# A top-2 mixture of experts on one core: tiles of 128 slots with one expert each become tiles of two 64-slot halves, each with its own expert

## The chip, the cores and the metric

The kernel runs on one core of a Trainium2 chip. The metric is the device time in microseconds (us) of one execution. Everything is computed in 32-bit floats; most matrix products, those of the experts among them, are plain fp32 products, each of which the trace shows as two weight loads and two matmul records.

The engines are named as the profile names them: PE (TensorE, matmul), PEld (its weight loads), DVE (VectorE), ACT (ScalarE), POOL (GpSimd), SP (SyncE, which here issues most DMAs). SBUF is the on-chip memory, PSUM the accumulator that PE writes. PEclk is the share of full TensorE clock that was granted.

## The reference

One layer of a decoder trunk: a gated linear recurrence and a differential attention over 1104 tokens (16 meta tokens, 64 sample tokens, 1024 prompt tokens), merged and projected, and then the part that the change is about, a mixture of 16 small MLPs. Each token goes to one group of four experts and, inside it, to the best two experts:

```python
g_idx = jnp.argmax(g_logits, axis=-1)
top_p, top_i = lax.top_k(e_prob, TOP_K)                 # TOP_K = 2, inside the chosen group of 4
gate = p_g * top_p / jnp.sum(top_p, axis=-1, keepdims=True)
eid = g_idx[..., None] * EXPERTS_PER_GROUP + top_i
h = jax.nn.silu(jnp.einsum('btd,edf->btef', x, w_gate)) * jnp.einsum('btd,edf->btef', x, w_up)
return jnp.einsum('btef,efd->btd', h * combine[..., None].astype(h.dtype), w_down)
```

`D_MODEL` is 1024 and the width of an expert 256, so an expert has 1024x256 numbers in each of `w_gate` and `w_up` and 256x1024 in `w_down`, 3 MB in all. 1104 tokens times two experts are 2208 assignments. Worked out from the reference's inputs, experts 0 to 15 get 144, 126, 82, 114, 209, 155, 153, 209, 114, 130, 162, 134, 114, 103, 117 and 142 of them.

## The kernel before

The program is a row of phases, each a block in which every engine has its own instruction stream: the first norm, the recurrence, prompt attention, sample attention, the merge, the output projection (`phase_output`), the routing (`phase_route`), the experts (`phase_experts`) and the copy of the results (`phase_results`). The change lies in the last but two and the last but one.

**Routing.** `phase_route` finds each token's two experts on DVE, counts the tokens of each expert, and gives every assignment a slot. A tile is 128 slots of one expert; an expert with n tokens gets n/128 tiles, rounded up. The arrays `token` (row to fetch), `dest` (row to add to), `slot_weight` (the gate, 0 in an empty slot), `expert` and `buffer` (expert of a tile, modulo 4) and `ends` (the number of tiles up to and with expert e) hold the plan. SP loads the weights of the first four experts meanwhile, and POOL gathers the rows of the first two tiles.

**A tile.** In `phase_experts` PE runs `step` for tile j (`par` = j modulo 2 picks the buffers):

1. the product for gate and up of tile j (L2208), 8 pieces of 128 rows by 512 columns, into PSUM bank 2 + par. It waits for `xt_done` (the turned rows are in SBUF) and for `weights_ready`;
2. the turn of tile j + 1 (L2185), 8 transposes;
3. the down product of tile j - 1 (L2195), 4 pieces of 512 columns, which ends with an increment of `y_made`;
4. the turn of the hidden values of tile j (L2179), which waits for `h_done`.

ACT follows with `silu` (L2235), `result` (L2241, half of the down product of the tile before, out of PSUM) and `hidden` (L2245); DVE with `hidden` (L2280, up times silu times gate), `place` (L2276, the turned rows to SBUF) and `result` (L2287). POOL gathers rows (L2086) and adds a tile's output rows to the running sum in DRAM (L2141). A token's two experts are in different tiles, and the additions of a tile wait for those of the tile before.

**Weights.** There are four buffers of expert weights. SP's program, L2121 to L2135, sets when a buffer is filled and when its content is announced. `say_ready(e)` waits until the three DMAs of expert e have landed and then raises `weights_ready` by one:

```python
for e in range(BUFFERS - 2):
    say_ready(e)
for e in range(BUFFERS, E):
    say_ready(e - 2)
    ends = sp.value_load(K["ends"][0:1, e - BUFFERS:e - BUFFERS + 1], min_val=0, max_val=SLOTS)
    sp.wait_ge(y_made, ends + 1)
    load_expert(sp, A, K, e, e % BUFFERS)
for e in range(E - 2, E):
    say_ready(e)
```

`y_made` starts at 1, so the wait is for the down product of the last tile of expert e - 4.

Tiles are run in pairs; with the counts above there are 25 tiles, so 26 run, the last one empty.

Of the kernel before, what the change touches and what calls it, by code (L numbers as in the profile page):

```python
# [49 lines left out]
SLOTS = (2 * TOK - E) // P + E + 1  # L50
# [5 lines left out]
FEWEST = -(-2 * TOK // P)  # L56
# [25 lines left out]
def constants():  # L82
# [40 lines left out]
    c["experts"] = np.broadcast_to(np.concatenate([np.arange(4, 0, -1), 128.0 * np.arange(9), np.arange(P)]).astype(np.float32), (P, 13 + P)).copy()  # L123
# [8 lines left out]
def build(nc, A, out):  # L132
    with ExitStack() as stack:
# [70 lines left out]
        K["expert"], K["buffer"], K["token"], K["dest"], K["ends"], K["before_last"] = (sb(n).bitcast(I32) for n in (SLOTS, SLOTS, SLOTS, SLOTS, E, 1))  # L204
        K["slot_weight"] = sb(SLOTS)
        top[0] = 0
# [1672 lines left out]
def phase_route(nc, A, K, sb, psum):  # L1879
# [3 lines left out]
    with ExitStack() as st:  # L1883
# [4 lines left out]
        bias, consts, strict, ones, tok, valid, emask = sb(20), sb(13 + P), sb(P), sb(P), sb(NT), sb(NT), sb(E, NT)  # L1888
# [7 lines left out]
        inc, cmp9, ntile, incl, excl, sm = sb(E, NT), sb(E, NT), sb(E), sb(E), sb(E), sb(NT, E)  # L1896
        lt, eid, eidb, step, last = sb(SLOTS, E), sb(SLOTS), sb(SLOTS), sb(SLOTS), sb(1)
# [4 lines left out]
        pri, steps128, jj, lanes = consts[:, 0:4], consts[:, 4:13], consts[:, 13:13 + SLOTS], consts[:, 13:13 + P]  # L1902
# [37 lines left out]
        def _(dve):  # L1940
# [42 lines left out]
            for j in range(2):  # L1983
                dve.tensor_tensor(OH[j].rearrange("p n (g e) -> p n g e", g=G), ohg.unsqueeze(3).to_broadcast([P, NT, G, PE_]),
                                  oh[j].unsqueeze(2).to_broadcast([P, NT, G, PE_]), ALU.mult)
# [20 lines left out]
            dve.tensor_tensor(cmp9, inc[:, :, NT - 1:NT].to_broadcast([P, E, NT]), steps128.unsqueeze(1).to_broadcast([P, E, NT]), ALU.is_gt)  # L2006
            D_()
            dve.tensor_reduce(ntile, cmp9, AX_X, ALU.add)
# [7 lines left out]
            dve.tensor_scalar(excl, excl, float(P), None, ALU.mult)  # L2016
# [41 lines left out]
            dve.tensor_tensor(lt, incl.unsqueeze(1).to_broadcast([P, SLOTS, E]), jj.unsqueeze(2).to_broadcast([P, SLOTS, E]), ALU.is_le)  # L2058
# [6 lines left out]
            dve.tensor_copy(K["ends"], incl)  # L2065

            dve.tensor_tensor(step[:, 0:SLOTS // 2 - 1], consts[:, 15:13 + SLOTS:2], incl[:, E - 1:E].to_broadcast([P, SLOTS // 2 - 1]), ALU.is_lt)
# [22 lines left out]
def load_expert(sp, A, K, e, b):  # L2090
# [6 lines left out]
def phase_experts(nc, A, K, sb, psum):  # L2097


    with ExitStack() as st:  # L2100
# [9 lines left out]
        hg, hT, Y = [sb(FF) for _ in range(2)], [sb(2, P) for _ in range(2)], [sb(D) for _ in range(2)]  # L2110
        block = st.enter_context(nc.Block())
        PAIRS = SLOTS // 2

# [58 lines left out]
        def _(pe):  # L2172
            def buffer_of(j):
                return pe.value_load(K["buffer"][0:1, bass.ds(j, 1)], min_val=0, max_val=BUFFERS - 1)
# [13 lines left out]
            def down(j, par, first, b):  # L2188
                pe.wait_ge(ht_done, j + 1)
                if not first:  # L2190
                    pe.wait_ge(y_act, j)
                    pe.wait_ge(y_dve, j)
                for n in range(2):
                    for k in range(2):
                        mm = pe.matmul(psum[:, 5 + n, :], hT[par][:, k, :], K["Wd"][:, bass.ds(2 * b + k, 1), 512 * n:512 * n + 512], start=(k == 0), stop=(k == 1))  # L2195
                mm.then_inc(y_made, 1)

            def step(i, par, first=False, end=False):
# [3 lines left out]
                e = pe.value_load(K["expert"][0:1, bass.ds(j, 1)], min_val=0, max_val=E - 1)  # L2202
# [29 lines left out]
        def _(act):  # L2232
# [13 lines left out]


            silu(0, 0)
# [113 lines left out]
```

## Time and profile before

| | us |
|---|---|
| three runs | 1891.2, 1893.44, 1904.81 |
| median | 1893.44 |
| the profiled execution, its own time | 1894.98 |
| its span in the trace | 1893.3 |

| engine | busy us | share of the span |
|---|---|---|
| PE | 1619.3 | 86% |
| DVE | 638.8 | 34% |
| ACT | 470.0 | 25% |
| POOL | 256.4 | 14% |

The experts' phase runs from about 1554 us to about 1864 us; after it come the last additions to the running sum and the copy of the results. In the rows, a line such as L2208 is line 2208 of the kernel before; x16 counts records, so a plain fp32 product counts twice; in brackets stands the idle time of that engine just before, and what ended it.

### The profile page before, as it was taken

To read this page: it belongs to the slowest core of one execution; us is meant where nothing else is said; L and a number is where in the kernel's file an instruction comes from. 1 tells how busy PE (TensorE), PEld (TensorE's weight loads), DVE (VectorE), ACT (ScalarE), POOL (GpSimd) and SP (SyncE) were. 2 spreads that over 40 slices of the span, in tenths; PEclk is the share of its full clock that TensorE was granted. 3 is DMA by queue.
4 is the path that set the end of the run, shared out by engine and by line. 5 is a ranking of instruction groups with operands and counts; after the bars stand their busy time and mean duration, and the time that the engine had idled before them with its cause. 6 is when DMAs were issued, how large, how long until landed. Compare 5 with 4: busy or idle time off the path is not lost. (4 is left out here: it accounts for less than half of the span.)

```text
span 1893.3 us, 25322 instructions
## 1 busy us (share of the span) xinstructions
PE 1619.3 (86%) x9005; PEld 1068.2 (56%) x9006; DVE 638.8 (34%) x1496; ACT 470.0 (25%) x1158; POOL 256.4 (14%) x455
## 2 busy tenths in 40 slices
PE   5998889966898989896576899999899829999993
PEld 4554445544465656554354788888678724444441
DVE  4345454454244544444231311111132241112210
ACT  2233333333233434343122211011132200111110
POOL 1000101011222222221322000000000001222211
PEclk8999899986898999998797999999999959999997
DMA  6001200000302020000983221111143294989755
GB/s 210 1 1 57 69 1 25 1 25 3 96 1 58 1 58 1 24 1 24 318 302 97 77 67 34 34 34 34 49 140 101 100 304 132 305 233 272 223 144 128
DMA packets 135893, 179.08 MB, mean 95 GB/s; under 512 B 9427, under 2 KB 106966, under 8 KB 135702
## 3 DMA queue, kind: packets, MB, share of 16 engines
q1 hardware_dynamic: 123126, 131.47, 21.8%
q0 software_dynamic: 12608, 44.05, 8.7%
q10 hardware_dynamic: 48, 2.10, 0.3%
q8 instruction: 68, 1.11, 0.3%
q14 instruction: 43, 0.35, 0.1%
HBM read 146.72 MB, written 35.32 MB: 96 GB/s over the span
## 5 line engine op out<-in xcount | busy, mean ns | idle before, releaser
L979 PE MATMUL psum<-branch_part,kept 128*128 128x384 f32 (+1 forms) x576 | 198.2, 499 | 1.5 <-DVE branch_part L1210 1.5
L2208 PE MATMUL psum<-moe_part,kept 128*128 x416 | 185.9, 600 | 5.9 <-DVE kept L2276 3.4
L979 PEld LDWEIGHTS psum<-branch_part,kept 128*128 128x128 f32 (+1 forms) x576 | 106.8, 190 | 75.4 <-issue 14.2
L487 PE MATMUL psum<-kept,branch_part 128*128 128x368 f32 x384 | 127.5, 489 | 8.1 <-PEq L224 5.1
L1644 PE MATMUL psum<-split 128*128 128x368 f32 x384 | 133.3, 347 | 0.0
L1638 PE MATMUL psum<-kept,merge_part 128*128 128x368 f32 x384 | 124.2, 476 | 9.6 <-DMA merge_part<-w_da_out 9.6
L2208 PEld LDWEIGHTS psum<-moe_part,kept 128*128 128x128 f32 x416 | 77.7, 192 | 95.7 <-issue 94.9
L492 PE MATMUL psum<-branch_part,kept 128*128 128x512 f32 (+1 forms) x288 | 129.3, 604 | 1.5 <-DVE kept L701 1.5
L1645 PE MATMUL psum<-split 128*128 128x368 f32 x384 | 126.9, 331 | 0.0
L1646 PE MATMUL psum<-split 128*128 128x368 f32 x384 | 126.6, 330 | 0.0
L1693 DVE TENSOR_TENSOR merge_part<-merge_part,psum 128x368 f32<-128x368 f32 x48 | 23.6, 534 | 252.8 <-ACT merge_part L1669 252.8
L487 PEld LDWEIGHTS psum<-kept,branch_part 128*128 128x128 f32 x384 | 74.2, 197 | 53.4 <-issue 10.5
L1638 PEld LDWEIGHTS psum<-kept,merge_part 128*128 128x128 f32 x384 | 72.9, 191 | 50.9 <-DMA merge_part<-w_da_out 10.0
L2195 PE MATMUL psum<-moe_part,kept 128*128 x208 | 93.7, 593 | 0.9 <-ACT kept L2245 0.9
L492 PEld LDWEIGHTS psum<-branch_part,kept 128*128 128x128 f32 (+1 forms) x288 | 54.2, 192 | 67.2 <-issue 64.9
L1669 ACT ACTIVATE merge_part<-psum 128x368 f32<-128x368 f32 x48 | 20.3, 474 | 276.1 <-PE psum L1646 276.1
L1002 PE MATMUL psum<-branch_part 128*128 128x512 f32 (+3 forms) x192 | 76.3, 514 | 0.0
L2280 DVE SCALAR_TENSOR_TENSOR kept<-kept,moe_part,psum 128x256 f32<-128x256 f32 x26 | 12.5, 481 | 186.7 <-ACT kept L2235 186.7
L1358 PE MATMUL psum<-kept,branch_part 128*128 128x128 f32 x256 | 45.5, 332 | 34.3 <-DMA branch_part<-cache_k 21.8
L1644 PEld LDWEIGHTS psum<-split 128*128 128x128 f32 x384 | 72.2, 188 | 2.9
L1645 PEld LDWEIGHTS psum<-split 128*128 128x128 f32 x384 | 72.1, 188 | 2.9
L1038 PE MATMUL psum<-branch_part 128*128 128x128 f32 (+2 forms) x360 | 60.2, 310 | 15.7 <-DVE branch_part L1210 14.1
(326 smaller groups left out, 2575.1 us busy)
## 6 DMA issues: line engine op xcount, KB each, us to landing
branch_part<-cache_k SPq DMA_DIRECT2D x64, 256.0 KB, 5.8
branch_part<-cache_v POOLq DMA_DIRECT2D x64, 256.0 KB, 5.2
moe_part<-w_gate SPq DMA_DIRECT2D x16, 1024.0 KB, 6.5
moe_part<-w_up SPq DMA_DIRECT2D x16, 1024.0 KB, 12.7
moe_part<-w_down SPq DMA_DIRECT2D x16, 1024.0 KB, 13.8
branch_part<-w_in SPq DMA_DIRECT2D x8, 1024.0 KB, 8.3
merge_part<-w_in SPq DMA_DIRECT2D x16, 512.0 KB
branch_part<-w_in SPq DMA_DIRECT2D x12, 512.0 KB
```

Source lines behind the costliest of these rows:

```text
L487: mm = pe.matmul(bank[:, 0:CH], Wb[0][:, k, c0:c0 + P], K["xT"][:, k, CH * i:CH * i + CH], start=(k == 0), stop=(k == KC - 1))
L492: mm = pe.matmul(bank[:ROWS[i], :], K["xT"][:, k, cols(i)], Wb[1][:, k, :], start=(k == 0), stop=(k == KC - 1))
L979: mm = pe.matmul(bank_of(("z", h, i))[:ROWS[i], 0:384], K["xT"][:, k, cols(i)], Wb[h % 2][:, k, :], start=(k == 0), stop=(k == KC - 1))
L1002: mm = pe.matmul(lg[m][:r, c:c + w], q, kT[h % 2][:, FIRST + c:FIRST + c + w], start=True, stop=True)
L1038: mm = pe.matmul(bank_of(("o", s, 0))[:r, 0:P], aT[:w, n, :r], v[h % 2][:w, 0 if n == i else n + 1, :], start=(n == 0), stop=(n == i))
L1358: mm = pe.transpose(psum[:, 3 + n % 2, P * h:P * h + P], Kp[b2][:, n % NPG, P * h:P * h + P], K["ident"])
L1638: pe.matmul(banks[2 + j], Wy[c % 2][:, k, P * j:P * j + P], src[:, k, chunk(n)], start=(k == 0), stop=(k == HEADS - 1))
L1644: pe.matmul(banks[j], wh[c % 2][:, k, ch], xh[:, k, chunk(n)], start=(k == 0), stop=False)
L1645: pe.matmul(banks[j], wh[c % 2][:, k, ch], xl[:, k, chunk(n)], start=False, stop=False)
L1646: mm = pe.matmul(banks[j], wl[c % 2][:, k, ch], xh[:, k, chunk(n)], start=False, stop=(k == KC - 1))
L2195: mm = pe.matmul(psum[:, 5 + n, :], hT[par][:, k, :], K["Wd"][:, bass.ds(2 * b + k, 1), 512 * n:512 * n + 512], start=(k == 0), stop=(k == 1))
L2208: mm = pe.matmul(psum[:, 2 + par, :], XT[par][:, k, :], K["GU"][:, bass.ds(KC * b + k, 1), :], start=(k == 0), stop=(k == KC - 1))
```

## The change

**The tile.** A tile still has 128 slots, but they are two halves (`groups`) of 64, and each half has an expert of its own. An expert with n tokens gets n/64 halves, rounded up, and the halves follow one another without a gap, so that an expert can end in the first half of a tile and the next begin in the second.

**The order of the experts.** They are taken in the order 0, 4, 8, 12, 1, 5, 9, 13, 2, 6, 10, 14, 3, 7, 11, 15. Neighbours are of different groups, and a token's two experts are of one group, so the two halves of a tile never hold the same token and a tile's rows can be added in one indirect DMA. By the counts above the halves per expert in this order are 3, 4, 2, 2, 2, 3, 3, 2, 2, 3, 3, 2, 2, 4, 3, 3, together 43.

**The products.** Each matmul of a tile becomes two: one with the weights (stationary side: the 64 turned rows) of slots 0 to 63 into PSUM partitions 0 to 63, one with slots 64 to 127 into partitions 64 to 127. The first reads the expert's weights in their buffer; the second reads a copy in `GU2` and `Wd2`, made per tile by ACT (`copy_gate`, 6 of the 8 rows of 512, two instructions) and DVE (`copy_up`, 2 of the 8 rows; `copy_down`, 2048 columns). The copies of a tile are made even where both halves have one expert.

**The plan.** `expert` and `buffer` have an entry per half, `ends` is the number of tiles up to and with the tile in which an expert ends.

```diff
+GROUPS = 2
+GROUP = P // GROUPS
+ENTRIES = (2 * TOK - 2) // GROUP + E
+SLOTS = -(-ENTRIES // (2 * GROUPS)) * 2
+NSTEP = -(-TOK // GROUP)
+CUT = 6
...
+            dve.tensor_scalar(ends, incl, 1.0 / GROUPS, 0.5 - 0.5 / GROUPS, ALU.mult, ALU.add)
...
-def load_expert(sp, A, K, e, b):
+def load_expert(sp, A, K, turn, b):
+
+    e = 4 * (turn % 4) + turn // 4
...
+        def second_of(e, j):
+
+            x = e.value_load(K["expert"][0:1, bass.ds(2 * j + 1, 1)], min_val=0, max_val=E - 1)
+            b = e.value_load(K["buffer"][0:1, bass.ds(2 * j + 1, 1)], min_val=0, max_val=BUFFERS - 1)
+            e.wait_ge(weights_ready, x + 1)
+            return b
...
             def down(j, par, first, b):
                 pe.wait_ge(ht_done, j + 1)
+                pe.wait_ge(down_copied, j + 1)
...
-                        mm = pe.matmul(psum[:, 5 + n, :], hT[par][:, k, :], K["Wd"][:, bass.ds(2 * b + k, 1), 512 * n:512 * n + 512], start=(k == 0), stop=(k == 1))
+                        pe.matmul(psum[0:64, 5 + n, :], hT[par][:, k, 0:64], K["Wd"][:, bass.ds(2 * b + k, 1), 512 * n:512 * n + 512],
+                                  start=(k == 0), stop=(k == 1))
+                        mm = pe.matmul(psum[64:128, 5 + n, :], hT[par][:, k, 64:128], Wd2[par][:, k, 512 * n:512 * n + 512],
+                                       start=(k == 0), stop=(k == 1))
...
+                pe.wait_ge(gate_copied, j + 1)
+                pe.wait_ge(up_copied, j + 1)
                 for k in range(KC):
-                    mm = pe.matmul(psum[:, 2 + par, :], XT[par][:, k, :], K["GU"][:, bass.ds(KC * b + k, 1), :], start=(k == 0), stop=(k == KC - 1))
+                    pe.matmul(psum[0:64, 2 + par, :], XT[par][:, k, 0:64], K["GU"][:, bass.ds(KC * b + k, 1), :],
+                              start=(k == 0), stop=(k == KC - 1))
+                    mm = pe.matmul(psum[64:128, 2 + par, :], XT[par][:, k, 64:128], GU2[par][:, k, :],
+                                   start=(k == 0), stop=(k == KC - 1))
...
+            def copy_gate(j, par, first=False):
+                b = second_of(act, j)
+                if not first:
+                    act.wait_ge(gu_done, j - 1)
+                for k in range(0, CUT, 3):
+                    ins = act.activation(GU2[par][:, k:k + 3, :], K["GU"][:, bass.ds(KC * b + k, 3), :], ACT.Copy)
+                ins.then_inc(gate_copied, 1)
...
             with act.Fori(1, PAIRS - 1) as i:
                 with act.If(i < last):
+                    copy_gate(2 * i + 2, 0)
                     silu(2 * i + 1, 1)
                     result(2 * i, 0, i)
                     hidden(2 * i + 1, 1)
+                    copy_gate(2 * i + 3, 1)
                     silu(2 * i + 2, 0)
...
+            def copy_up(j, par, first=False):
+                b = second_of(dve, j)
+                if not first:
+                    dve.wait_ge(gu_done, j - 1)
+                dve.tensor_copy(GU2[par][:, CUT:KC, :], K["GU"][:, bass.ds(KC * b + CUT, KC - CUT), :]).then_inc(up_copied, 1)
+
+            def copy_down(j, par, first=False):
+                b = second_of(dve, j)
+                if not first:
+                    dve.wait_ge(y_made, j)
+                dve.tensor_copy(Wd2[par], K["Wd"][:, bass.ds(2 * b, 2), :]).then_inc(down_copied, 1)
...
             with dve.Fori(1, PAIRS - 1) as i:
                 with dve.If(i < last):
+                    copy_up(2 * i + 2, 0)
                     hidden(2 * i + 1, 1)
                     place(2 * i + 2, 0, False)
                     result(2 * i, 0, i)
+                    copy_down(2 * i + 2, 0)
```

SP's program is not changed.

On PE, in the loop of `phase_experts`, the step of a tile stood before as follows (the first two of the eight pieces of the gate and up product; REGISTER_ALU and ISA are waits and address registers):

```order
L2205 REGISTER_ALU
L2206 REGISTER_ALU
L2208 ISA
L2208 MATMUL psum<-moe_part,kept 128x512
L2208 ISA
L2208 MATMUL psum<-moe_part,kept 128x512
```

The same place in the changed kernel (`kept` holds `XT` and `GU2`, `moe_part` the expert buffers):

```order
L2232 REGISTER_ALU
L2233 REGISTER_ALU
L2237 ISA
L2237 MATMUL psum<-moe_part,kept 64x512
L2239 MATMUL psum<-kept 64x512
L2237 ISA
L2237 MATMUL psum<-moe_part,kept 64x512
L2239 MATMUL psum<-kept 64x512
```

Each product with 128 output rows has become two neighbours with 64 each, the second from the copy.

On ACT, the first half of the loop's body stood before as follows (`silu`, `result`, `hidden`):

```order
L2234 ISA
L2235 ACTIVATE kept<-psum 128x256
L2240 REGISTER_ALU
L2241 ACTIVATE kept<-psum 128x512
L2245 ACTIVATE kept<-psum 128x256
```

The same place in the changed kernel (L2133 loads a register, L2134 is the wait for `weights_ready`, L2284 the copy, L2267 is `silu`):

```order
L2133 TENSOR_LOAD moe_part
L2133 ISA x2
L2134 REGISTER_ALU
L2282 REGISTER_ALU
L2284 ISA
L2284 ACTIVATE kept<-moe_part 128x1536
L2284 ISA
L2284 ACTIVATE kept<-moe_part 128x1536
L2267 ACTIVATE kept<-psum 128x256
L2272 REGISTER_ALU
L2273 ACTIVATE moe_part<-psum 128x512
L2277 ACTIVATE kept<-psum 128x256
```

The copy for tile j + 1, with its wait for the weights of that tile's second half, now stands on ACT in front of `silu` of tile j; `copy_up` stands on DVE in front of `hidden` of tile j in the same way.

## Rows read from the trace of the kernel before

**Rows 1.** Costliest groups of the page: line engine op, count | busy, mean ns | idle
```profile
L2208 PE MATMUL psum<-moe_part,kept 128*128 x416 | 185.9, 600 | 5.9 <-DVE kept L2276 3.4
L2195 PE MATMUL psum<-moe_part,kept 128*128 x208 | 93.7, 593 | 0.9 <-ACT kept L2245 0.9
```

**Rows 2.** The chain that ended last, in order of time: start, duration, what
```profile
1708.74 6.87 PE psum L2208 x16
...
1811.69 6.95 PE psum L2208 x16
...
1834.57 2.50 issue
```

**Rows 3.** Timeline of one tile's step: start us, duration us, engine, line
```profile
1605.24 0.38 PE L2179 MATMUL psum<-kept 128*128 128x128 f32 x2
...
1605.52 7.13 PE L2208 MATMUL psum<-moe_part,kept 128*128 x16
...
1612.48 1.04 PE L2185 MATMUL psum<-kept,moe_part 128*128 128x128 f32 x8
1612.68 0.39 ACT L2235 ACTIVATE kept<-psum 128x256 f32<-128x256 f32 x1 [6.28 <-PE psum L2208]
1613.22 0.48 DVE L2280 SCALAR_TENSOR_TENSOR kept<-kept,moe_part,psum 128x256 f32<-128x256 f32 x1 [6.99 <-ACT kept L2235]
...
1613.62 1.22 DVE L2276 COPY kept<-psum 128x1024 f32<-128x1024 f32 x1
```

**Rows 4.** Timeline of sample attention, PE alone; 128*32 is 32 output rows
```profile
931.83 3.46 PE L1358 MATMUL psum<-kept,branch_part 128*128 128x128 f32 x16 [4.01 <-DMA branch_part<-cache_k]
935.22 1.07 PE L1372 MATMUL psum<-branch_part 128*32 128x512 f32 x8
936.11 0.46 PE L1377 MATMUL psum<-branch_part 128*32 128x80 f32 x16
```

**Rows 5.** The same, products of 128 columns with 32 output rows
```profile
1013.76 1.96 PE L1401 MATMUL psum<-branch_part 128*32 128x128 f32 x64 [0.69 <-ACT branch_part L1463]
1015.53 0.40 PE L1404 MATMUL psum<-branch_part 80*32 80x128 f32 x8
```

**Rows 6.** Timeline of the recurrence, PE alone: 128 output rows, then 64
```profile
300.82 5.11 PE L487 MATMUL psum<-kept,branch_part 128*128 128x368 f32 x16
305.86 0.48 PE L509 MATMUL psum<-branch_part 128*64 128x64 f32 x4
```

**Rows 7.** Groups of ACT by form: copies from SBUF to SBUF
```profile
L1658 ACT ACTIVATE split<-merge_part 128x2048 fp32r<-128x2048 f32 x8 | 15.3, 1913 | 3.0 <-DMA merge_part<-w_da_out 3.0
...
L1817 ACT ACTIVATE output_split<-kept 128x1024 fp32r<-128x1024 f32 x8 | 8.3, 1043 | 0.0
```

**Rows 8.** Timeline of SP: the DMAs of an expert's weights as they are issued
```profile
1594.04 0.37 SPq L2093 DMA_DIRECT2D moe_part<-w_gate  x1
...
1595.08 1.48 SPq L2094 DMA_DIRECT2D moe_part<-w_down  x1
...
1628.38 0.37 SPq L2093 DMA_DIRECT2D moe_part<-w_gate  x1
```

**Rows 9.** Timeline at the start of the experts' phase, tiles 0 and 1
```profile
1559.08 8.96 PE L2208 MATMUL psum<-moe_part,kept 128*128 x16 [1.71 <-DVE kept L2276]
...
1568.49 0.48 DVE L2280 SCALAR_TENSOR_TENSOR kept<-kept,moe_part,psum 128x256 f32<-128x256 f32 x1 [9.86 <-ACT kept L2235]
...
1571.17 7.13 PE L2208 MATMUL psum<-moe_part,kept 128*128 x16 [1.70 <-DVE kept L2276]
```

**Rows 10.** Windows: PE, PEld, DVE, ACT, POOL busy; PEclk, DMA share, GB/s
```profile
931.80:934.60 2.80, 2.77 (x13) 2.30 (x13) 0.69 (x1) 0.60 (x1) 1.32 (x3) 0.50 1.02 399
1605.40:1617.00 11.60, 11.60 (x36) 5.65 (x35) 2.31 (x4) 1.26 (x4) 2.56 (x2) 1.00 1.06 345
1648.40:1650.40 2.00, 2.00 (x6) 0.93 (x5) 0.77 (x1) 0.00 (x0) 0.00 (x0) 1.00 0.04 14
```

**Rows 11.** DMA issues of the page: KB each, median us from issue to landing
```profile
moe_part<-w_down SPq DMA_DIRECT2D x16, 1024.0 KB, 13.8
```

More of the change, by code:

```diff
@@ L122, in constants @@
     c["strict"] = (s < t).astype(np.float32)
-    c["experts"] = np.broadcast_to(np.concatenate([np.arange(4, 0, -1), 128.0 * np.arange(9), np.arange(P)]).astype(np.float32), (P, 13 + P)).copy()
+    c["experts"] = np.broadcast_to(np.concatenate([np.arange(4, 0, -1), [-1.0], float(GROUP) * np.arange(1, NSTEP), np.arange(P)]).astype(np.float32), (P, 4 + NSTEP + P)).copy()
     c["token_id"] = (np.array(COL)[None, :] + np.arange(P)[:, None]).astype(np.float32)
@@ L203, in build @@
         K["X"] = [sb(D) for _ in range(2)]
-        K["expert"], K["buffer"], K["token"], K["dest"], K["ends"], K["before_last"] = (sb(n).bitcast(I32) for n in (SLOTS, SLOTS, SLOTS, SLOTS, E, 1))
+        K["expert"], K["buffer"], K["token"], K["dest"], K["ends"], K["before_last"] = (sb(n).bitcast(I32) for n in (GROUPS * SLOTS, GROUPS * SLOTS, SLOTS, SLOTS, E, 1))
         K["slot_weight"] = sb(SLOTS)
+        K["Wd2"], K["Y"] = [sb(2, D) for _ in range(2)], [sb(D) for _ in range(2)]
         top[0] = 0
@@ L1895, in phase_route @@
         M, pre, tot = sb(NT, E), sb(NT, E), sb(E, NT)
-        inc, cmp9, ntile, incl, excl, sm = sb(E, NT), sb(E, NT), sb(E), sb(E), sb(E), sb(NT, E)
-        lt, eid, eidb, step, last = sb(SLOTS, E), sb(SLOTS), sb(SLOTS), sb(SLOTS), sb(1)
+        inc, over, ntile, incl, excl, sm = sb(E, NT), sb(E, NSTEP), sb(E), sb(E), sb(E), sb(NT, E)
+        lt, eid, eidb, step, last, ends = sb(GROUPS * SLOTS, E), sb(GROUPS * SLOTS), sb(GROUPS * SLOTS), sb(GROUPS * SLOTS), sb(1), sb(E)
         sl, tile, within, tok1, spare = sb(2, NT), sb(2, NT), sb(2, NT), sb(NT), sb(1)
@@ L2064, in _ @@
             dve.tensor_copy(K["expert"], eid)
-            dve.tensor_copy(K["ends"], incl)
-            dve.tensor_tensor(step[:, 0:SLOTS // 2 - 1], consts[:, 15:13 + SLOTS:2], incl[:, E - 1:E].to_broadcast([P, SLOTS // 2 - 1]), ALU.is_lt)
+            dve.tensor_scalar(ends, incl, 1.0 / GROUPS, 0.5 - 0.5 / GROUPS, ALU.mult, ALU.add)
+            D_()
+            dve.tensor_scalar(ends, ends, ROUND, None, ALU.add)
+            D_()
+            dve.tensor_scalar(ends, ends, -ROUND, None, ALU.add)
+            D_()
+            dve.tensor_copy(K["ends"], ends)
+            dve.tensor_tensor(step[:, 0:SLOTS // 2 - 1], groups[:, 2 * GROUPS::2 * GROUPS], incl[:, E - 1:E].to_broadcast([P, SLOTS // 2 - 1]), ALU.is_lt)
             D_()
@@ L2109, in phase_experts @@
         X, XT = K["X"], [sb(KC, P) for _ in range(2)]
-        hg, hT, Y = [sb(FF) for _ in range(2)], [sb(2, P) for _ in range(2)], [sb(D) for _ in range(2)]
+        hg, hT, Y = [sb(FF) for _ in range(2)], [sb(2, P) for _ in range(2)], K["Y"]
+        GU2, Wd2 = [sb(KC, 512) for _ in range(2)], K["Wd2"]
+        gate_copied, up_copied, down_copied = sem("gate_copied"), sem("up_copied"), sem("down_copied")
         block = st.enter_context(nc.Block())
         PAIRS = SLOTS // 2
+        def second_of(e, j):
[3 more added lines that the diff above has]
+            return b
         def last_pair(e):
@@ L2252, in _ @@
             hidden(1, 1)
+            copy_gate(3, 1)
             silu(2, 0)
```

36 lines of the change are left out of this document (24 added, 12 removed).

## The prediction

> **What bounds the kernel now.** The page's costliest groups come first: the two products of the experts are 186 and 94 us of PE time and PE waited 6.8 us for them in all [rows 1], so the experts' phase is PE from end to end. The chain of waits says the same: from 1708.74 to 1811.69 us it is nine tiles of PE alone, so a tile costs 102.95 / 9 = **11.44 us**; one stop of 2.50 us stands at the loop's exit, where four unused iterations are skipped [rows 2]. In the timeline of one step [rows 3] I read who must be on time. Gate and up take 6.87 us of PE, 16 records of 0.43; `silu` ends and `hidden` starts within the turn and the down product, 1.02 us from 1612.68 to 1613.70. ACT and DVE are idle for over 6 us before, so there is room for copies, if they stand there.
>
> **Removed: tiles.** In halves the experts end at 3, 7, 9, 11, 13, 16, 19, 21, 23, 26, 29, 31, 33, 37, 40, 43. 43 halves are 22 tiles, where 26 run now: 4 x 11.44 = **-45.8 us**. Two unused iterations in place of four are skipped: half of 2.50, **-1.2**.
>
> **The pairs.** Each product becomes two with 64 output rows, and the question is whether PE runs both at once. The trace has such products: the scores of sample attention put four products of 512 columns, 32 output rows each, next to one another. Eight records start at 935.22, and the next line's at 936.11 [rows 4]: 0.89 us, where one after the other they would take 8 x 0.43 = 3.44. With 128 columns, 64 records take 1.77 us to the next line's start [rows 5] against 64 x 0.11 = 6.9. So four run at once at nearly full rate, each with its own moving data, and I take two of 64 to do the same. 0.89 against 2 x 0.43 leaves 0.03 us at the start of a group, two groups per tile: 22 x 0.06 = **+1.3**. Upper end: 0.015 us in every one of the 24 rounds of a tile, +8.
>
> In the Trainium skill, "TensorE: Matmul & The Clock Gate", Part 3, three products of 32 output rows and 512 columns gain 2.38, not 3. By that share the two products of a tile would take 10.3 / 0.79 = 13.0 us instead of 10.3, an estimate, and 22 tiles 59 us more, to about 1957. The trace here shows 3.44 / 0.89 = 3.9 of 4 [rows 4], and the sum goes by the trace.
>
> **Changes of form.** PE goes from 64 output rows to the full turns and back, four times a tile. From L487 (16 records of 368 columns, 0.307 each by 512 columns in 0.43, so 4.92) to the first 64-row product it is 5.04 us [rows 6]: 0.1 per change. 88 x 0.1 = **+8.8**, from 0 (hidden by nothing else to do) to 17.
>
> **Copies in a normal tile.** ACT copies 1536 numbers per partition twice; between 1.04 for 1024 and 1.91 for 2048 [rows 7] that is 1.48 each, 3.0 a tile. It starts after `hidden` of the tile before, when PE starts gate and up, and ends 3.5 us into its 6.9. DVE copies 3072 columns, at most 3 x 1.22 = 3.7 us [rows 3], and with `result` (half of 1.22) before them this ends some 4.5 us into the same 6.9. Cost nothing; without that cover they would cost 22 x 3 = 66. The copies' own waits for buffers (`gu_done` of two tiles back) are long past.
>
> **The wait that the copies bring.** This decides. ACT's copy for tile J waits in the queue ahead of `silu` of tile J - 1, and it waits for the announcement of the expert x of J's second half. SP announces x only after it has waited for the down product of the last tile of x - 3 and has issued the load of x + 1. Counting experts by turn, the first tile J of x = 4 to 14 is 5, 6, 8, 9, 10, 11, 13, 14, 15, 16, 18; the last tile of x - 3 is 3, 4, 5, 6, 7, 9, 10, 11, 12, 14, 15. In step J - 1 PE runs the down product of J - 2. Where the last tile of x - 3 is J - 3 (x = 6, 7, 8, 10, 11, 12, 14), that product ended before step J - 1 began. SP's issue of 2.5 us and ACT's 3.0 end before gate and up do: nothing lost. Where it is **J - 2**, that is **x = 4, 5, 9, 13**, `silu` of J - 1 cannot run until the down product of J - 2, behind its own gate and up, is over. PE then stands still at L2179. From that product's end: SP issues three DMAs, 1594.04 to 1596.56 [rows 8], 2.5; announcement 0.1; copies 3.0; `silu` and `hidden` 1.0 [rows 3]; then from `hidden`'s end at 1568.97 to the next gate and up at 1571.17, 2.2, for the place and PE's register loads [rows 9]. Sum 8.8, less 0.1 that passes there now: **8.7**. It cannot be zero: the order SP, ACT, DVE, PE is a chain.
>
> While PE stands for 8.7 us its clock falls. After a wait of 4.01 us, 16 records of 128 columns took 3.39 us to the next start [rows 4], against 16 x 0.11 = 1.74, so 1.65 lost; the granted clock was 0.50, 1.2 GHz, there and 1.00, 2.4 GHz, in a tile's step [rows 10]. The first gate and up of the phase took 8.96 against 7.13 later [rows 9], 1.8 lost. I take 1.8, from 0 to 2.5. So a stall costs 10.5 and four **+42.0**. Lower end: if SP's issue and half of the copies are covered, 4 x 4.7 = 19; upper end: an issue of 7 us as at a full queue, 4 x 15 = 60.
>
> **Weights in time.** An expert takes 1 us to the last issue and 13.8 to its landing [rows 11], 14.8. A step moves 3.15 MB of weights and 0.52 twice for gather and addition, 4.2 MB, and the busy stretch moves 345 GB/s [rows 10]: 12.1 us, against 11.9 for the new step. Loads come after the down products of tiles 1, 3, 4, 5, 6, 7, 9, 10, 11, 12, 14, 15. The fourth of a run of four, issued at 1628.38, was in by 1648.4 [rows 8, 10], 20.0 us; a third one takes some 18. A copy can start up to 7.1 us into a step (7.0 for gate and up, 3.1 of slack behind it, less 3.0), so one step and 7.1 us, 19.0, are given for x = 8 and 12, the thirds. Just in time: nothing.
>
> **The sum.** -45.8 - 1.2 + 1.3 + 8.8 + 42.0 = **+5.1**. The profiled execution took 1894.98 (span 1893.3), 1.5 over the median of 1893.44; like for like that is 1900.1, and at the median 1898.5, so **1899**. Routing (arrays of 50 halves, two more small operations) hides under the first loads, which end at about the same time as now.
>
> **Rivals.**
>
> 1. *The stalls are not there or small.* For it: ACT and DVE idle over 6 us before each `silu` [rows 3]. Against it: the copies stand in front of `silu` in one queue. With none, 1893.4 - 45.8 - 1.2 + 10.1 = 1856.5, faster; with 4.7 each, about 1875. Chance 0.22.
> 2. *Weights land late*, slower. Four loads in a row already make a queue, and 12.1 us a load is over a step. It decides from a landing of over 19 us after issue: with 4 us more, at x = 8 and 12 and once again behind one of them, each 4 + 1 for the clock, 15 us: 1914. Against it: the four stalls give the queue time. Chance 0.13.
> 3. *Pairs overlap less than fully.* By the 0.015 us in every round, +8 in place of 1.3, 1906, and more if two pieces of 64 share worse than four of 32. Against it: rows 4 and 5 as a whole. Chance 0.12, half of it over 1%. By the rule of the Trainium skill weighed above ("TensorE: Matmul & The Clock Gate", Part 3) this rival would be at about 1957.
> 4. *Pairs do not overlap at all* with 64 rows: 22 x 10.3 = 227 more, 2126. Only pieces of 32 rows were seen side by side, so 0.03.
>
> That more than 22 tiles run would need other counts; the loads before stand at the tiles that these counts give, so I leave it out.
>
> **How the numbers follow.** The forecast has 0.50, with its own range 1884 to 1914: one change of form per tile more or less (9), stalls 2 us more or less each (8). About 1% is what a measurement of this kernel can tell from no change, so the bounds are 1874.5 and 1912.4. Faster: 0.02 of the forecast, 0.18 of rival 1, 0.20. Slower: 0.05 of the forecast, 0.07 of rival 2, 0.07 of rival 3, 0.03 of rival 4, 0.22. Within: 0.58. The range runs from 1865, which leaves most of rival 1 without stalls outside, to 1925, which leaves rival 4 and the far end of rival 3 outside.
>
> **What would show it.** 22 `silu` and a chain with tiles of about 11.9 us; L2237 and L2239 together 6.9 us per tile, starting some ns apart; four idle stretches of PE of 8 to 9 us, in steps 4, 5, 10 and 15, put down to DVE or ACT, with SP's three issues at their start and PEclk at 0.50 behind them; `copy_gate` 1.5 us each. Wrong if PE stands at other tiles, if a stall's first part is a landing, or if a tile without a stall is over 12.5 us.

## The result and the profile after

The changed kernel takes **1907.28 us** (median; 1898.75 to 1914.55), beside it the kernel before 1896.13: a ratio of **1.0053**, 95% interval 1.0037 to 1.007, or 10 to 11 us more. The profiled execution took 1909.74 us, its span is 1908.1. The prediction was 1899, with 1865 to 1925 around it: no change that matters, from 47 us saved and 52 given back. The measured time is 0.5% over the kernel before, which is small but clear of the noise, and 8 us over the forecast.

The costliest groups of the page, in its section 5: out<-in, count | busy, mean ns | idle before, and what ended it. L2208 of before [rows 1] is now L2237 (first half) and L2239 (second half), L2195 is L2219 and L2221, L2235 is L2267 (`silu`), L2280 is L2325 (`hidden`), L2276 is L2321 (the place), L2093 and L2094 are L2107 and L2108 (the loads). The turn of the rows, L2185 of before, is L2208 here, and the turn of the hidden values, L2179 of before, is L2202. SP announces an expert at L2146. In the kernels with another order of groups most of these lines are one further down:

```profile
L2237 PE MATMUL psum<-moe_part,kept 128*64 x352 | 166.5, 629 | 13.5 <-issue 11.9
L2239 PE MATMUL psum<-kept 128*64 128x512 f32 x352 | 166.8, 628 | 0.0
...
L2284 ACT ACTIVATE kept<-moe_part 128x1536 f32 x44 | 62.8, 1477 | 120.7 <-SPq L2146 79.3
```

352 records each, 16 a tile: 22 tiles. Both halves' products are busy in the same time. L2284 is ACT's copy of the weights of a tile's second half, two instructions a tile of three of the eight rows each, 1.48 us each; ACT waited 79.3 us for SP's announcement (L2146) ahead of it. In the waits of the experts' phase (us in total, times, longest) the new one of PE, for `hidden`, has four entries:

```profile
ACT kept L2284 <- SPq L2146: 79.3, 12, 18.0
...
PE psum L2202 <- DVE kept L2325: 27.1, 4, 6.9
```

The timeline of the first of the four, in step 4, without the weight loads (start us, duration us):

```profile
1624.63 0.59 PE L2221 MATMUL psum<-moe_part,kept 128*64 128x512 f32 x1
1625.26 0.37 SPq L2107 DMA_DIRECT2D moe_part<-w_gate  x1
...
1626.30 1.57 SPq L2108 DMA_DIRECT2D moe_part<-w_down  x1
1628.07 2.86 ACT L2284 ACTIVATE kept<-moe_part 128x1536 f32 x2 [13.86 <-SPq L2146]
...
1630.83 0.36 ACT L2267 ACTIVATE kept<-psum 128x256 f32<-128x256 f32 x1
...
1631.89 0.69 PE L2202 MATMUL psum<-kept 128*128 128x128 f32 x2 [6.67 <-DVE kept L2325]
...
1634.51 1.11 PE L2237 MATMUL psum<-moe_part,kept 128*64 x1 [1.93 <-issue]
```

Read it from the top: the down product of tile 3 ends at 1625.2, only then SP issues three DMAs and announces an expert, only then ACT copies (2.86 us), then `silu`, which had its input since about 1620.5, then `hidden`, then PE's turn of the hidden tile after 6.67 us of rest, and 1.93 us more until gate and up. The chain that ended last goes the same way in the last of the four (start, duration, what):

```profile
1792.39 1.66 SPq L2108
1794.52 1.18 issue
1795.70 1.47 ACT kept L2284
1798.22 1.00 DVE kept L2321
1799.22 2.31 issue
1801.53 1.11 PE psum L2237
```

Windows of the trace (PE, PEld, DVE, ACT, POOL busy; PEclk, DMA share, GB/s): at the end of the stop, behind it, and in a tile without one. A PEclk of 0.50 is 1.2 GHz, 1.00 is 2.4 GHz, and 0.79 a stretch with both:

```profile
1631.90:1634.50 2.60, 0.68 (x2) 0.28 (x2) 2.60 (x3) 0.38 (x1) 0.17 (x1) 0.50 1.07 386
1634.60:1643.00 8.40, 8.40 (x32) 2.63 (x32) 0.10 (x1) 0.00 (x0) 2.53 (x2) 0.79 0.68 162
...
1672.20:1684.20 12.00, 12.00 (x61) 4.43 (x60) 4.22 (x6) 4.02 (x6) 2.85 (x2) 1.00 0.96 285
```

**The account.** I take the starts of each tile's gate-and-up product (the first L2208, now L2237, of the tile). From the first tile's to the last tile's it is 289.5 us before and 300.0 after (1564.28 to 1864.31). A tile without a stop takes 12.01 us after, where it took 11.44. The steps that are longer, in us:

| step | takes | beyond 12.01 | what it is |
|---|---|---|---|
| 4 | 21.00 | 8.99 | stop |
| 5 | 23.73 | 11.72 | 1.82 clock of the stop before, 9.90 stop |
| 6 | 13.91 | 1.90 | clock |
| 10, 11 | 20.98, 14.28 | 8.97, 2.27 | stop, clock |
| 15, 16 | 22.04, 13.94 | 10.03, 1.93 | stop, clock |

The clock's part is how much longer gate and up took, from the start of its first record to that of its last, than the 6.49 of a tile without a stop (8.31, 8.39, 8.76, 8.42). So: 4 tiles fewer, -45.8; 21 x 0.565 = +11.9 for the pairs; +37.9 for the four stops and +7.9 for the clock behind them; -1.8 at the loop's exit (0.8 in place of 2.6); +0.5 at the start. Together +10.6, measured +10.5. The spans differ by 14.8; of the other 4.3, 4.0 is there at about 1504 us already, ahead of the experts' phase. Single profiled executions differ there by themselves: in the traces of the runs below the first gate and up starts between 1557.3 and 1566.5 us.

### The profile page after: what moved, and what is told of

The parts are those of the page before. It is cut to its first block and busy times, and to the rows that moved or that the text cites. A ratio compares the mean times of both kernels' runs of the same rounds, so it can differ in the third digit from the quotient of the medians.

```text
span 1908.1 us, 26665 instructions
## 1 busy us (share of the span) xinstructions
PE 1602.6 (84%) x9397; PEld 1027.3 (54%) x9398; DVE 673.3 (35%) x1532; ACT 526.8 (28%) x1191; POOL 249.7 (13%) x447
## 5 line engine op out<-in xcount | busy, mean ns | idle before, releaser
L985 PE MATMUL psum<-branch_part,kept 128*128 128x384 f32 (+1 forms) x576 | 203.1, 508 | 1.9 <-DVE branch_part L1216 1.5
L2237 PE MATMUL psum<-moe_part,kept 128*64 x352 | 166.5, 629 | 13.5 <-issue 11.9
L2239 PE MATMUL psum<-kept 128*64 128x512 f32 x352 | 166.8, 628 | 0.0
L2237 PEld LDWEIGHTS psum<-moe_part,kept 128*64 128x64 f32 x352 | 49.0, 145 | 112.5 <-issue 112.5
L2284 ACT ACTIVATE kept<-moe_part 128x1536 f32 x44 | 62.8, 1477 | 120.7 <-SPq L2146 79.3
L2219 PE MATMUL psum<-moe_part,kept 128*64 x176 | 80.2, 598 | 0.8 <-ACT kept L2277 0.8
L2221 PE MATMUL psum<-moe_part,kept 128*64 128x512 f32 x176 | 80.3, 598 | 0.0
```

Of the source, the lines that this page charges most:

```text
L985: mm = pe.matmul(bank_of(("z", h, i))[:ROWS[i], 0:384], K["xT"][:, k, cols(i)], Wb[h % 2][:, k, :], start=(k == 0), stop=(k == KC - 1))
L2219: pe.matmul(psum[0:64, 5 + n, :], hT[par][:, k, 0:64], K["Wd"][:, bass.ds(2 * b + k, 1), 512 * n:512 * n + 512], start=(k == 0), stop=(k = ...
L2221: mm = pe.matmul(psum[64:128, 5 + n, :], hT[par][:, k, 64:128], Wd2[par][:, k, 512 * n:512 * n + 512], start=(k == 0), stop=(k == 1))
L2237: pe.matmul(psum[0:64, 2 + par, :], XT[par][:, k, 0:64], K["GU"][:, bass.ds(KC * b + k, 1), :], start=(k == 0), stop=(k == KC - 1))
L2239: mm = pe.matmul(psum[64:128, 2 + par, :], XT[par][:, k, 64:128], GU2[par][:, k, :], start=(k == 0), stop=(k == KC - 1))
```

## The experiments

Two theories stood against each other at first: the time went back to the four stops, which come from one rule (an expert's first tile stands two behind the last tile of the expert three turns earlier); or the price is in the pairs and copies of every tile, and the stops are only where it shows. Each run moves one of these. Ratios are to the kernel before.

### The same tiles in another order of groups

Experts are taken in the order of groups 2, 3, 0, 1. The tiles are as many, and no expert of turns 4 to 14 has its first tile J so close that the last tile of the expert three turns earlier is J - 2:

```diff
-    e = 4 * (turn % 4) + turn // 4
+    e = 4 * ((turn + 2) % 4) + turn // 4
```

(The table of one-hot rows, by which the slots are given out, is written in two slices to the same order.)

> The changed kernel with the groups taken in the order 2, 3, 0, 1 instead of 0, 1, 2, 3, so that the experts' turns are 8, 12, 0, 4, 9, 13, 1, 5 and so on. Halves end at 2, 4, 7, 11, 14, 16, 18, 21, 24, 26, 28, 31, 34, 37, 39, 43: still 22 tiles, as many loads as densely, but the first tile J of each expert x of turns 4 to 14 is at least three tiles behind the last tile of x - 3. Theory (the announcement stands behind the down product of the last tile of x - 3, and the copies in front of silu): no stall, the four that cost 45.8 us in the changed kernel's trace go, about 1862 us. Rival (weights land late, by bandwidth): loads are as many and as dense, stalls stay, 1900 or more.

Measured: 1862.99 us (1854.19 to 1865.07), ratio 0.9806 (0.9771 to 0.9841). Each step from 1 to 18 takes 12.01 or 12.02 us. The page's group and a window of 12 us:

```profile
L2238 PE MATMUL psum<-moe_part,kept 128*64 x352 | 157.4, 600 | 4.2 <-DVE kept L2322 1.8 <-ACT kept L2285 1.7 <-issue 0.7
```

```profile
1750.00:1762.00 12.00, 12.00 (x60) 4.45 (x58) 4.39 (x5) 4.35 (x6) 2.57 (x2) 1.00 1.02 306
```

Same pairs, same copies (4 us of ACT in the window), and PE does not stop; the mean product falls from 629 to 600 ns, as the clock stays up. The 44 us between the medians of this and of the changed kernel are the four stops and their clock, 45.8 by the table above. This is the version to keep, **33 us faster than before**.

### SP announces one expert earlier

SP, before it waits for a free buffer, announces expert e - 1 and not only e - 2. It must then wait for the load of e - 1 to land before it issues the next one.

```diff
-            for e in range(BUFFERS - 2):
+            for e in range(BUFFERS - 1):
...
-                say_ready(e - 2)
+                say_ready(e - 1)
...
-            for e in range(E - 2, E):
+            for e in range(E - 1, E):
```

> The changed kernel; SP announces expert e - 1, not e - 2, before it waits for the down product that frees the buffer of expert e. Order of experts and tiles unchanged. Theory: the stalls at the tiles of experts of turns 4, 9 and 13 go; that of turn 5 stays, because its load is issued only after the down product of tile 3: it lands 11 us later, copies to 14, silu, hidden and registers to 17.3 against a step of 12.0, so 5 us and 2 for the clock. 45.8 - 7 = 39 us less than the changed kernel, about 1868. Rival (SP now waits for each landing, so loads follow one another 11 to 15 us apart and weights come late): at least as many stalls as before, 1900 or more.

Measured: 1884.9 (1876.92 to 1888.1), ratio 0.992 (0.9888 to 0.9952): between the two. Three of the four stops are gone, so the late announcement is their cause. The expert of turn 5 still stops PE (step 5: 21.96, and 2.24 for the clock behind it, 12.2 in all where 7 were expected), and small ones are new: steps 9, 10, 11, 15 and 16 take 1.7 to 2.5 us more, 9.5 together. SP's timeline:

```profile
1627.60 0.37 SPq L2107 DMA_DIRECT2D moe_part<-w_gate  x1
...
1643.07 0.37 SPq L2107 DMA_DIRECT2D moe_part<-w_gate  x1
...
1679.40 0.37 SPq L2107 DMA_DIRECT2D moe_part<-w_gate  x1
...
1695.05 0.37 SPq L2107 DMA_DIRECT2D moe_part<-w_gate  x1
```

The loads go one by one, 15.5 us from issue to issue (1643.07 - 1627.60), which is over a step of 12.01; a run of them falls behind. One of the small stops, PE and ACT:

```profile
1709.25 2.86 ACT L2284 ACTIVATE kept<-moe_part 128x1536 f32 x2 [8.44 <-SPq L2146]
...
1712.02 0.36 ACT L2267 ACTIVATE kept<-psum 128x256 f32<-128x256 f32 x1
...
1715.69 1.02 PE L2237 MATMUL psum<-moe_part,kept 128*64 x1 [1.81 <-issue]
```

`hidden` comes at about the time at which PE needs it, so almost nothing is lost at L2202. But PE's sequencer stood at that wait, and its register loads for the next tile, which it otherwise does ahead, now stand in the open: 1.81 us. The trace has them on the sequencer from 1713.19 to 1715.14, right behind the end of `hidden`. And behind it the granted clock was 0.53, nearly all of it at 1.2 GHz (window 1715.70 to 1718.00), though PE's longest rests in these two steps were 1.61 and 1.81 us.

### The early announcement in the order without stops

Both edits together: is it the serial loads in themselves that cost, or the catching up behind the stop that was left?

> The rotated order with SP announcing expert e-1 instead of e-2 ahead of each wait for a buffer. No expert's first tile is at J-2 here, so the early announcement can repair nothing; it can only delay the next issue until the load ahead has landed, so that loads go one after the other (15.4 us from issue to issue). Theory (the leftover stalls of e2_early come from these serial loads): where first tiles follow each other at one tile (12.01 us) the weights come late, by 3 us a step, some 5 to 15 us in all, 1870 to 1878. Rival (they came from catching up after the stall that was left): 1863, no stall.

Measured: 1863.1 (1858.01 to 1863.89), ratio 0.9819 (0.9777 to 0.986), the same as without it. Steps 9 and 14 take 12.65 and 12.58, all others 12.01. So serial loads alone cost 1.2 us; the theory's 5 to 15 was wrong. This points to the stop in step 5, behind which the loads ran close, as the source of what was left over in the run before; that is not shown, as I did not isolate how one becomes the other.

### ACT and DVE copy behind what PE waits for

`copy_gate` of tile J stands behind `silu` of J - 1, and `copy_up` behind `hidden`, in the changed kernel's order of experts:

```diff
-                    copy_gate(2 * i + 2, 0)
                     silu(2 * i + 1, 1)
+                    copy_gate(2 * i + 2, 0)
...
-                    copy_up(2 * i + 2, 0)
                     hidden(2 * i + 1, 1)
+                    copy_up(2 * i + 2, 0)
```

> The changed kernel with ACT's copy for tile j + 1 behind silu of tile j and DVE's copy_up behind hidden of tile j, not in front of them. Theory: the four stalls stay at the same tiles, but silu, hidden and the register loads no longer come after the copies: from the down product's end 2.65 for SP, 3.0 for the copies, then gate and up at once, 5.7 against 0.4 now, so 5.3 in place of 9.0 each, with about 1.9 for the clock as before: 29 in place of 45.8, 17 us less than the changed kernel, about 1890. A tile without a stall stays at 12.0. Rival (the stall is a landing): silu's place makes no difference to it beyond 1 us each, 1903 or more.

Measured: 1890.47 (1889.39 to 1897.98), ratio 0.9983 (0.9966 to 1.0). The stops are at the same four steps, but smaller: 17.55, 20.54, 17.50 and 17.83, and the steps behind them 14.89, 14.80 and 14.61. One of them:

```profile
1620.52 2.86 ACT L2284 ACTIVATE kept<-moe_part 128x1536 f32 x2 [6.95 <-SPq L2146]
...
1623.60 1.11 PE L2237 MATMUL psum<-moe_part,kept 128*64 x1 [5.47 <-ACT kept L2284]
```

PE now waits at L2237 for the copy itself, not at L2202: 5.5 us in place of 6.7 + 1.9. `silu` and the register loads have gone under the announcement and the copy. These are the two parts of the sum that can be hidden without touching SP: 12 us over four stops, by the steps 45.8 - 33.7. So a good fourth of the price comes from the copy's place ahead of `silu`, and the rest from the late announcement and the copy itself. The expectation had 17 us for this. The median, 16.8 us under the changed kernel's, is at its 1890 all the same, but 4.7 us of that are not in the stops, so this much of the agreement is luck.

The stops themselves are 15.4 us shorter in all (22.5 in place of 37.9), but the clock behind them costs 11.2 in place of 7.9: gate and up took 9.40, 9.37, 9.29 and 9.09. From 1623.60 to 1629.00 the granted clock was 0.50 (1.2 GHz), behind a rest of 5.47 us.

### An order with two stops

Groups in the order 0, 3, 2, 1, by the rule two experts whose first tile is only two behind that last tile (J - 2), in steps 6 and 11:

```diff
-    e = 4 * (turn % 4) + turn // 4
+    e = 4 * (-turn % 4) + turn // 4
```

> The changed kernel with the groups in the order 0, 3, 2, 1. The turns are experts 0, 12, 8, 4, 1, 13, 9, 5 and so on; 22 tiles, loads as many as before. By the same count (last tile of x - 3 against first tile J of x) exactly two experts, those of turns 6 and 10, have it at J - 2. Theory: two stalls of 11.4 us with their clock, none elsewhere: 1863 + 23 = 1886 us. Rival (the order 2, 3, 0, 1 was faster for another reason, such as a better spread of the loads): 1863 or 1907, or stalls at other tiles.

Measured: 1892.67 (1884.48 to 1895.88), ratio 0.9981 (0.9964 to 0.9998). There are **three** stops: in steps 6 (20.82) and 11 (21.52), and in step 2 (20.91):

```profile
1600.93 0.37 SPq L2108 DMA_DIRECT2D moe_part<-w_gate  x1
...
1603.80 2.86 ACT L2285 ACTIVATE kept<-moe_part 128x1536 f32 x2 [14.00 <-SPq L2147]
...
1607.49 0.69 PE L2203 MATMUL psum<-kept 128*128 128x128 f32 x2 [6.60 <-DVE kept L2326]
```

My count began at the expert of turn 4. The one of turn 3 is announced behind the same wait (for the last tile of turn 0), and here its first tile is 3 and that last tile 1: J - 2 again. The rule held at all three places, and I had looked at too few. Three stops of 11 us on 1863 give 1896, and 1892.67 was measured. In the changed kernel the expert of turn 3 has its first tile at 4 and is no stop.

### Single products of 128 rows

Both products of a tile are one of 128 rows again, with the order and the copies of the changed kernel; the second half then uses the first half's expert, so that part of the result is left out.

```diff
-                    pe.matmul(psum[0:64, 2 + par, :], XT[par][:, k, 0:64], K["GU"][:, bass.ds(KC * b + k, 1), :],
-                              start=(k == 0), stop=(k == KC - 1))
-                    mm = pe.matmul(psum[64:128, 2 + par, :], XT[par][:, k, 64:128], GU2[par][:, k, :],
+                    mm = pe.matmul(psum[:, 2 + par, :], XT[par][:, k, :], K["GU"][:, bass.ds(KC * b + k, 1), :],
                               start=(k == 0), stop=(k == KC - 1))
```

(and the same in `down`)

> The changed kernel with every pair of 64-row products made one product of 128 rows with the first half's expert; plan, copies and waits are kept. The second half of a tile is computed with the first half's expert, so that part of the result is left out. Theory (0.565 us per tile more than before are the pairs: four changes of form and the start of a group): a tile is 11.45 us again, the four stalls are unchanged, 22 x 0.565 = 12 us less than the changed kernel, about 1895. Rival (the 0.565 us come from the two more waits and the copies on ACT and DVE): no change, 1907.

Measured: 1894.75 (1890.71 to 1905.6), ratio 0.9992 (0.9974 to 1.001). Tiles without a stop are back at 11.40 to 11.67 us, 11.5 in the mean, and all four stops are there (20.53, 23.88, 20.66, 21.63). The turns' starts are 11.4 apart:

```profile
1585.17 1.04 PE L2208 MATMUL psum<-kept,moe_part 128*128 128x128 f32 x8
1596.56 1.04 PE L2208 MATMUL psum<-kept,moe_part 128*128 128x128 f32 x8
```

So the pairs cost some 0.5 us a tile, 12 in all (1.0053 - 0.9992 of 1896), and the stops don't need them. The copies and the two more waits, which this run keeps, cost under 0.1 us a tile.

### Where in a tile the pairs cost: one product at a time

On the order without stops, only gate and up in single products, and then only down. In the single products the second half takes the first half's expert, so that part of the result is left out:

> On the rotated order (no J-2 stall, tile 12.01 us). The gate-and-up product alone goes back to one product of 128 rows (8 instead of 16 a tile; the second half then uses the first half's expert, so that part of the result is left out); the down products stay pairs. Theory (0.57 us a tile are four changes of form at about 0.14 each: into and out of each of the two products with halves): two changes are left, tile 11.73, 1863 - 6 = 1857 us. Rival (the price goes with the number of 64-row pairs, 8 of gate-and-up and 4 of down): two thirds go, tile 11.63, 1855.

> The other way round, on the rotated order: the down products are single ones of 128 rows (4 instead of 8 a tile), the gate-and-up product stays pairs. Theory (four changes of form): tile 11.73 us, 1857 us, the same as with gate-and-up alone. Rival (price by pairs): a third goes, tile 11.82, 1859.

Starts of the turns, with gate and up in single products:

```profile
1612.57 1.04 PE L2209 MATMUL psum<-kept,moe_part 128*128 128x128 f32 x8
1624.27 1.04 PE L2209 MATMUL psum<-kept,moe_part 128*128 128x128 f32 x8
```

and with down in single products:

```profile
1588.24 1.09 PE L2209 MATMUL psum<-kept,moe_part 128*128 128x128 f32 x8
1599.95 1.10 PE L2209 MATMUL psum<-kept,moe_part 128*128 128x128 f32 x8
```

11.70 and 11.71 us a tile: each gives back 0.31 of the 0.57, though gate and up has 8 pairs and down 4. The price goes by changes of form, not by pairs, and is **0.15 us a change** (0.31 / 2). The changed kernel's own trace shows it at all four places of a tile:

```profile
1589.48 0.64 PE L2237 MATMUL psum<-moe_part,kept 128*64 x1
...
1596.51 1.09 PE L2208 MATMUL psum<-kept,moe_part 128*128 128x128 f32 x8
...
1597.54 0.64 PE L2219 MATMUL psum<-moe_part,kept 128*64 x1
...
1601.13 0.44 PE L2202 MATMUL psum<-kept 128*128 128x128 f32 x2
...
1601.49 0.64 PE L2237 MATMUL psum<-moe_part,kept 128*64 x1
```

From start to start the four parts take 7.03, 1.03, 3.59 and 0.36 us. In the kernel before they take 6.87, 0.87, 3.44 and 0.22 (tile at 1639.91): each is some 0.15 us longer now.

The whole kernels: 1851.37 (ratio 0.977, 0.9729 to 0.9811) and 1850.53 (0.9753, 0.9711 to 0.9795), some 6 us lower than 1857; from first to last tile the trace has 247.9 and 247.8 us against 253.1, so 5 of the 12 us that the spans differ by are in the tiles, and the other 7 lie ahead of the phase, which these edits do not touch.

### Two changes of form a tile in place of four

On the order without stops, PE takes gate and up, down, then the turn of tile j + 2 (the buffer it would turn into is free only so) and the turn of the hidden tile:

```diff
-                if not end:
-                    turn(i + par, 1 - par)
                 if before is not None:
                     down(j - 1, 1 - par, first, before)
+                if not end:
+                    pe.wait_ge(xt_done, j + 2)
+                    turn(i + 1, par)
                 turn_hidden(j, par)
```

> The kernel with the groups in the order 2, 3, 0, 1 (1863 us), and on PE the down product right behind gate and up, the turn of tile j + 2 behind it, and then the turn of the hidden values: two changes of form between 64 and 128 output rows per tile in place of four, all products and transposes kept. Theory (a change of form costs 0.15 us): a tile 12.01 - 0.30 = 11.71 us, 22 x 0.3 = 6.6 us less, about 1856. Rival (the 0.565 us are a cost inside the paired products): tile 12.01, 1863.

Measured: 1898.84 (1894.39 to 1904.05), ratio 1.0022 (1.0006 to 1.0038), 36 us over the order it started from. No step is at 11.7; the shortest regular ones are 12.04, and most are 13 to 17. PE in one of them:

```profile
1642.48 1.07 PE L2209 MATMUL psum<-kept,moe_part 128*128 128x128 f32 x8 [1.31 <-DMA moe_part<-normed,moe_part]
...
1646.43 1.11 PE L2238 MATMUL psum<-moe_part,kept 128*64 x1 [2.67 <-issue]
...
1661.42 0.64 PE L2238 MATMUL psum<-moe_part,kept 128*64 x1 [0.23 <-issue]
```

The turn waits for its gather (1.31 us), which was needed a step later until now; behind it the register loads and the loop's turn stand in the open, 2.67; and the gate and up at 1646.43 then runs 9.47 us instead of 6.49, with a granted clock of 0.50 (1.2 GHz) up to 1652.40. A lateness of 1.3 us has cost 7.0. The edit moved a transfer's due time, and I had only counted forms. The other long steps I did not take apart, and whether two changes of form would save their 0.3 us in an order that keeps the gather's slack is open.

One thing this trace does show is that the price needs a change of form. Here the down product stands right behind gate and up, 64 rows behind 64:

```profile
1637.12 0.59 PE L2238 MATMUL psum<-moe_part,kept 128*64 x1
...
1637.55 0.59 PE L2220 MATMUL psum<-moe_part,kept 128*64 x1
```

From the last round of gate and up to the first of down it is 0.43 us, the time of any round. So what costs is the change, and not the start of another group of pairs.

### The halves' products apart

On the order without stops, all eight products of the first half, then all eight of the second:

```diff
                 for k in range(KC):
                     pe.matmul(psum[0:64, 2 + par, :], XT[par][:, k, 0:64], K["GU"][:, bass.ds(KC * b + k, 1), :],
                               start=(k == 0), stop=(k == KC - 1))
+                for k in range(KC):
                     mm = pe.matmul(psum[64:128, 2 + par, :], XT[par][:, k, 64:128], GU2[par][:, k, :],
                                    start=(k == 0), stop=(k == KC - 1))
```

> The kernel with the groups in the order 2, 3, 0, 1 (1863 us), and in gate and up all eight products of the first half before all eight of the second, in place of alternating. If PE runs only neighbours in program order side by side, the first eight and the second eight take 6.9 us each and a tile 18.8 us: 22 x 6.9 = 151 more, 2014. If it starts a product of the other half past those that wait for their own columns, the time stays at 1863.

Measured: 1979.94 (1978.87 to 1981.02), ratio 1.0439 (1.0405 to 1.0472). A tile takes 17.21 us, 5.2 more. PE's timeline:

```profile
1636.92 5.79 PE L2238 MATMUL psum<-moe_part,kept 128*64 x13
1642.13 0.65 PE L2241 MATMUL psum<-kept 128*64 128x512 f32 x1
1642.55 0.59 PE L2238 MATMUL psum<-moe_part,kept 128*64 x1
...
1643.47 5.75 PE L2241 MATMUL psum<-kept 128*64 128x512 f32 x13
```

The second half's first record starts when thirteen of the first half's sixteen have started (the others at 1642.55, 1642.98 and 1643.41), and not before. PE does start it ahead of three records that stand before it in the program, but no further ahead. So the two halves run side by side only where they stand next to each other in the program: 7.03 us to the next work's start in pairs, 12.24 (1636.92 to 1649.16) apart. Strictly one after the other would have been 2014, and the small overlap is the rest.

## Why the prediction was right

**The tiles, right.** 22 tiles, 352 records of each half; -45.8 is arithmetic, and the exit gave 1.8 (predicted 1.2).

**The four stops, right in place, order and nearly in size.** Steps 4, 5, 10 and 15, put down to DVE, with SP's three issues at their start. Predicted 8.7 each; 8.97 to 10.03 by the steps, 9.5 in the mean. The parts: SP and the announcement 2.8 from the down product's end (2.6), copies 2.9 (3.0), `silu` and `hidden` up to L2202 1.0 (1.0), and from there to the next gate and up 2.6 in step 4 (2.2), of which 1.93 lie behind the turn of the hidden tile. The two longer ones, steps 5 and 15, end where the program's loop goes round, and there PE's "issue" is 0.8 us longer (2.71 for 1.93); I had one number for both. The order 2, 3, 0, 1 removes all four and 44 us: shown.

There was luck in the list of places. It began at the expert of turn 4, though the rule holds for turn 3 as well. Here turn 3 has its first tile at 4 and the last tile of turn 0 is 1, three apart, so nothing was missed; in the order 0, 3, 2, 1 the same list missed a stop.

**The clock, right.** 1.8 predicted, 1.82 to 2.27 measured; PEclk 0.50 at the end of the stop and 0.79 in the window behind it.

**The pairs, right in kind.** The products of both halves start 7 to 25 ns apart and a round takes 0.43 us, as for 128 rows [rows 3]. The share of 2.38 in 3 that the Trainium skill gives ("TensorE: Matmul & The Clock Gate", Part 3) would have meant 13.0 us for a tile's two products, by the prediction's estimate; the trace has 7.03 and 3.59 from the start of each to that of the next work (the tile at 1589.48). Rivals 3 and 4 fall.

**Changes of form, under-sized.** This is the term that was off: 0.1 each, measured 0.15, with the 1.3 for the starts of groups inside it. 10.1 was predicted for both, 12.4 measured. I took 0.1 from one single change [rows 6], read up to the start of the first 64-row product. The same stretch costs 0.09 here (0.20 from the last turn, at 1597.34, to the first down product, for 0.11), and another 0.05 stands behind it, in a first round of 0.48 for 0.43, which my reading left out. The Trainium skill ("TensorEngine Tiling (Array Packing)", Key Properties) says that a change of mode drains TensorE; a cost at each change and none without one agree with it, but no row shows the drain itself.

**Weights in time, right.** No step of the changed kernel is longer than 12.01 but those of the table, the first and the loop's exit. Rival 2 falls. The reason that was given against it, that the stops give the queue time, was not needed: in the order without stops the weights are in time too.

**The sum.** +5.1 predicted, +10.5 measured in the phase: 3.8 of stops and clock (45.8 for 42.0), 1.8 of pairs and forms (11.9 over 21 steps for 10.1), 0.5 at the start, less 0.6 at the exit. Of the 8.8 us by which the median lies over the sum, 2.7 more are that before stood at 1893.44 when I predicted and at 1896.13 beside the changed kernel; under 1 us is left over.

Rival 1 was the one that the first view of idle time spoke for: ACT busy a fourth of the span, over 6 us idle before each `silu`. It was wrong because the room was there before the announcement, and the copy can't start until then. Its place ahead of `silu` made this 12 us dearer, and without it 34 of the 46 us were still there.

The range was 60 us wide. All misses but that of the loop's exit went the same way, towards slower, and they fit into it.

## What to carry to other kernels

Where an engine takes on a new piece of work that waits for something, ask first when what it waits for can come, and then what stands behind it in that engine's queue. Here the copies waited for an announcement that stood behind another engine's wait and DMA issues, and `silu`, and with it PE, waited behind the copies; moving `silu` ahead gave back 12 of 46 us, and an order in which the wait is over in time gave back all. Then list, for every tile, which event releases the wait and whether it has passed by then; the list showed that four tiles of 22 pay and that in another order of the same work none does. The kernel in that order is 33 us faster than the one before. Begin that list at the first item that goes through the wait, not at the first one that the loop handles.

## What was not expected of the hardware

- Lateness of PE is not paid at its own size. `hidden` that came just in time cost 1.81 us (register loads that PE's sequencer otherwise does ahead) and then a granted clock of 0.53 up to 1718.00; a gather 1.31 us late cost 7.0 in all.
- Two products of 64 rows run side by side at the full rate of each (gate and up 7.03 us to the turn's start, 6.96 before [rows 3]), but only as near neighbours in the program; eight and eight in a row took 12.24. There a product started ahead of three records that stand before it in the program.
- A change between 64 and 128 output rows costs PE 0.15 us, whichever product it surrounds, and between two groups of 64 rows that follow each other nothing is lost (0.43 us, as for any round).
- A shorter rest of PE did not mean a cheaper clock behind it: 1.8 to 2.3 us behind the changed kernel's stops, 2.6 to 2.9 behind those that were 3.4 to 4.3 us shorter (ACT and DVE copying later).
